# Four small loads moved from ScalarE's queue to SyncE's, the sink loads moved behind a weight slab, and one projection tile computed in another order

## The reference

```python
for i in range(DEPTH):                      # 2 layers
    h = rmsnorm(x, norm_w[i])
    if i % 2 == 0:                          # attention, 4 key/value groups of 4 heads
        q, k, v, g = split(h @ w_attn_in)   # q, k are normalised per head
        p = softmax_with_sink(q @ k.T, attn_sinks)
        out = (p @ v * silu(g)) @ w_attn_out
    else:                                   # SSM: uses a_log, dt_bias, d_skip
        out = mamba2(h, ..., dt_bias, a_log, d_skip, ...) @ w_ssm_out
    x = x + out
```

## Time and profile before

| | before |
|---|---|
| median of 3 runs (range) | 1024.51 us (1024.32 to 1026.81) |
| profiled execution | 1027.62 us |
| span, first to last instruction | 1024.7 us |
| PE matmul busy | 980.9 us (96%) |
| DVE, ACT, POOL busy | 581.2, 466.9, 365.8 us |
| mean granted TensorE clock | 0.988 of full speed |

### The profile page before, as it was taken

One profiled execution on the slowest core, in us unless ns is written; L12 is line 12 of the kernel. 1 busy time (PEld: TensorE's weight loads), 2 busy tenths in 40 slices (PEclk: granted clock), 3 DMA queues, 4 the chain that ended last, 5 costly groups with the idle time before them and its releaser, 6 DMA issues.

```text
span 1024.7 us, 18539 instructions
## 1 busy us (share of the span) xinstructions
PE 980.9 (96%) x7372; PEld 902.1 (88%) x7372; DVE 581.2 (57%) x1433; ACT 466.9 (46%) x819; POOL 365.8 (36%) x275
## 2 busy tenths in 40 slices
PE   8999999999999999999997999999999999999988
PEld 7988899989998899978986889998799978997867
DVE  5114431354224431356685787966889577986772
ACT  5324623365134623366444364343552445526453
POOL 4240233113330233115533335534354244443610
PEclk9999999999999999999998999999999999999999
DMA  6351221242233222101423715247242563416303
GB/s 198 101 155 62 83 83 53 85 157 65 66 103 141 84 83 59 73 21 42 148 86 87 226 44 157 83 111 205 62 136 84 148 186 82 137 47 207 92 11 98
DMA packets 144117, 106.35 MB, mean 104 GB/s; under 512 B 10258, under 2 KB 135364, under 8 KB 143840
## 3 DMA queue, kind: packets, MB, share of 16 engines
q1 hardware_dynamic: 115032, 92.24, 29.0%
q10 hardware_dynamic: 29000, 12.94, 4.8%
HBM read 92.44 MB, written 16.79 MB: 107 GB/s over the span
## 4 chain that ended last, share of the span: by engine, by line
PE 79%; DVE 10%; issue 4%; DMA 3%; ACT 2%; POOL 2%; ACTq 0%; SPq 0%; DVEq 0%; POOLq 0%
PE pp L1202 19%; PE pp L1204 19%; PE pp L1203 18%; PE pS L1318 3%; DMA w_raw_buf<-in_w_attn_in 2%; PE pS L1542 2%; DVE cv L1914 2%; PE pO L1364 1%; PE pO L1363 1%; PE pO L1535 1%; PE pO L1531 1%; PE pT_ L1521 1%; PE pO L1482 1%; POOL w_lo_raw L608 1%; DVE z L2056 1%
## 5 line engine op out<-in xcount | busy, mean ns | idle before, releaser
L608 POOL TENSOR_TENSOR w_lo_buf<-w_raw_buf,w_hi_buf 128x512 fp32r<-128x512 f32 x214 | 288.0, 1377 | 503.0 <-ACT w_hi_buf L689 272.0
L1202 PE MATMUL pp<-h_hi,w_hi_buf 128*128 128x280 f32 (+1 forms) x1248 | 379.6, 304 | 7.8 <-POOL w_lo_buf L608 2.9
L1204 PE MATMUL pp<-h_hi,w_lo_buf 128*128 128x280 f32 (+1 forms) x1248 | 364.1, 292 | 0.0
L1203 PE MATMUL pp<-h_lo,w_hi_buf 128*128 128x280 f32 (+1 forms) x1248 | 363.5, 291 | 0.0
L1202 PEld LDWEIGHTS pp<-h_hi,w_hi_buf 128*128 128x128 f32 x1248 | 236.7, 190 | 19.0 <-issue 11.7
L1203 PEld LDWEIGHTS pp<-h_lo,w_hi_buf 128*128 128x128 f32 x1248 | 236.4, 189 | 4.6 <-issue 4.1
L1204 PEld LDWEIGHTS pp<-h_hi,w_lo_buf 128*128 128x128 f32 x1248 | 236.4, 189 | 0.0
L689 ACT ACTIVATE w_hi_buf<-w_raw_buf 128x2048 fp32r<-128x2048 f32 (+1 forms) x55 | 104.1, 1892 | 38.7 <-DMA w_raw_buf<-in_w_ssm_in 16.9
L1700 DVE TENSOR_TENSOR x<-x,pp 128x272 f32<-128x272 f32 (+3 forms) x128 | 56.4, 440 | 80.3 <-PE pp L1204 79.4
L1202 PE MATMUL pp<-og_hi,w_hi_buf 128*128 128x280 f32 (+2 forms) x256 | 76.2, 298 | 1.8 <-DVE og_lo L1821 1.1
L1204 PE MATMUL pp<-og_hi,w_lo_buf 128*128 128x280 f32 (+2 forms) x256 | 75.2, 294 | 0.0
(11 more groups left out here) (334 smaller groups left out, 1730.0 us busy)
## 6 DMA issues: line engine op xcount, KB each, us to landing
w_raw_buf<-in_w_attn_in SPq DMA_DIRECT2D x16, 1024.0 KB, 5.2
w_raw_buf<-in_w_ssm_in SPq DMA_DIRECT2D x16, 1024.0 KB, 5.4
w_raw_buf<-in_w_attn_out SPq DMA_DIRECT2D x8, 1024.0 KB, 5.1
s_in<-in_state_ssm SPq DMA_DIRECT2D x32, 256.0 KB, 4.2
out<-s_in SPq DMA_DIRECT2D x32, 256.0 KB, 3.0
seg<-a_scratch ACTq DMA_DIRECT2D x16, 512.0 KB, 4.1
w_raw_buf<-in_w_ssm_out SPq DMA_DIRECT2D x8, 1024.0 KB, 5.6
w_raw_buf<-in_w_attn_in SPq DMA_DIRECT2D x8, 512.0 KB, 5.9
```

Source lines behind the costliest of these rows:

```text
L608: ins = pool.tensor_tensor(low_buf(n)[:, piece], raw[n % RAW_SLOTS][:, piece], high_buf(n)[:, piece].bitcast(F32), ALU.subtract)
L1202: pe.matmul(dst, hi[:, k, cols], a_hi[:, k, tk], start=(k == 0), stop=False)
L1203: pe.matmul(dst, hi[:, k, cols], a_lo[:, k, tk], start=False, stop=False)
L1204: mm = pe.matmul(dst, lo[:, k, cols], a_hi[:, k, tk], start=False, stop=(k == depth - 1))
```

## The change

The two loads of `d_skip` and those of `dt_bias` and `a_log` leave ACT's program and stand in SP's, in the loop over the groups at group 1, behind the load of slab 7. On SP, the cached values of group 0 and slab 3 are now ahead of the sinks and sink rows. On POOL, the subtraction of the value columns of slab 0 waits for all eight blocks of activations. On PE, the first half of the value tile runs its 16 matmuls with the high weight first, then waits for the low part, then runs the 8 matmuls with the low weight.

```diff
+            def load_ssm_scalars():
+                for half in range(2):
+                    src = d_skip[0, :].rearrange("(t e) -> e t", e=2)[half]
+                    sp.dma_start(dskip[64 * half:64 * half + 64, :], src.partition_broadcast(64),
+                                 allow_slow_non_contiguous=True).then_inc(s_late, 16)
+                sp.dma_start(dtb[:, :], dt_bias.rearrange("a h -> h a"),
+                             allow_slow_non_contiguous=True).then_inc(s_late, 16)
+                sp.dma_start(alog[:, :], a_log.rearrange("a h -> h a"),
+                             allow_slow_non_contiguous=True).then_inc(s_late, 16)
...
+            load_cache(0, 1)
+            load_slabs(4)
             sp.dma_start(sinks[:, :], attn_sinks[0, :].partition_broadcast(P)).then_inc(s_small, 16)
...
-            load_cache(0, 1)
 
             for s in range(GROUPS):
+                if s == 1:
+                    load_slabs(slab_no[("out", 0, 1)] + 1)
+                    load_ssm_scalars()
                 load_slabs(slab_no[("gate", s, 1)] + 1)
...
                 if i:
-                    pool.wait_ge(h_ready, KM - 2)
+                    pool.wait_ge(h_ready, KM)
...
-            for half in range(2):
-                src = d_skip[0, :].rearrange("(t e) -> e t", e=2)[half]
-                act.dma_start(dskip[64 * half:64 * half + 64, :], src.partition_broadcast(64),
-                              allow_slow_non_contiguous=True).then_inc(s_late, 16)
-            act.dma_start(dtb[:, :], dt_bias.rearrange("a h -> h a"),
-                          allow_slow_non_contiguous=True).then_inc(s_late, 16)
-            act.dma_start(alog[:, :], a_log.rearrange("a h -> h a"),
-                          allow_slow_non_contiguous=True).then_inc(s_late, 16)
             norm_scale(0)
...
                 if (kind, s, tile) == ("kv", 0, 1):
                     pe.wait_ge(w_hi, 1)
-                    pe.wait_ge(w_lo, 1)
                     pe.wait_ge(x_ready, KM)
...
-                for k in range(depth):
+                high_first = (kind, s, tile, half) == ("kv", 0, 1, 0)
+                if high_first:
+                    for k in range(depth):
+                        pe.matmul(dst, hi[:, k, cols], a_hi[:, k, tk], start=(k == 0), stop=False)
+                        pe.matmul(dst, hi[:, k, cols], a_lo[:, k, tk], start=False, stop=False)
+                    pe.wait_ge(w_lo, 1)
+                    for k in range(depth):
+                        mm = pe.matmul(dst, lo[:, k, cols], a_hi[:, k, tk], start=False, stop=(k == depth - 1))
+                for k in range(0 if high_first else depth):
```

## The result

| | before | after |
|---|---|---|
| median (range): 4 runs before, 3 after | 1024.84 us (1024.32 to 1026.81) | 1013.84 us (1013.11 to 1014.47) |
| ratio (95% interval) | 1 | 0.9893 (0.9877 to 0.9908) |
| profiled execution, its span | 1027.62, 1024.7 us | 1013.84, 1011.5 us |
| mean granted TensorE clock | 0.988 | 0.993 |

A further run of the changed kernel took 2417.61 us, more than twice the others for a reason that the record does not show, and is left out of the table (with it the median is 1014.15). The forecast was 1015.5 us, with a spread of 1013.5 to 1018 and a range that goes to 1020.

A forecast was written before the change was run, and what follows sets the result against it. PE was taken as the bound from 72 us on, with gains only before 68 us: 2.28 + 1.49 + 3.08 + 1.33 + 0.86 = 9.04 us off the 1024.5 median gives 1015.5, spread 1013.5 to 1018, range to 1020.

The forecast's parts named there:

- Gap 1: PE's 2.16 us idle before the last activation block at 24.27; POOL waiting for eight blocks was to gain 2.28 us.
- High-first: Value tile's high-weight matmuls first: costs nothing and hides POOL's later low part, for which PE would otherwise wait 1.7 us.
- The slow half tile: Half tile from 25.18 to 29.86, behind the first gap, at the lower clock: 4.68 us would become 3.19, gain 1.49.
- Gap 2: PE's 2.92 us wait at 52.90 for slab 2's low part; moving the small loads off ACT was to gain 3.08.
- the slow stretch: Twelve matmuls from 52.90 to 55.83, behind the wait for slab 2: 2.93 us would become 1.60, gain 1.33.
- gap 3: PE's 0.70 us wait at 67.51 for slab 3's low part; slab 3 ahead of the sinks was to gain 0.86.
- The rival that queues take turns: Slab 2's late landing is not d_skip's doing, so only 0.86 us is won: 1025.6 us; chance 0.06.
- The rival that the small loads block slab 8: On SP the small loads land one after another, making slab 8 43.4 us late: 1058.9 us, slower; chance 0.05.
- the cover of 37.0: SP's queue may be held from 107.5 to 144.5 us before PE needs slab 8; each microsecond beyond costs one.
- The clock falling anyway: Rival: the start still has gaps and slow matmuls cost 1.49 or also 1.33: 1017.0 or 1018.3 us; chance 0.11.

The follow-up runs named there:

- run seven: Changed kernel, but POOL starts the value columns' low part after six blocks, as before: 1018.38 us, ratio 0.9933.
- Run six: Changed kernel, but PE waits for the low part before the value tile's first matmul, products in the old order: 1017.31 us, ratio 0.9926.
- run three: Kernel before with only SP's order changed, cached values and slab 3 ahead of the sinks: 1023.95 us, ratio 0.9989.
- run one: Kernel before with only the four small loads moved from ACT to SP behind slab 7: 1018.45 us, ratio 0.9932.
- nine: Changed kernel with only dt_bias and a_log (64 elements) back on ACT's queue: 1013.55 us, one run.
- twelve: Changed kernel once more, unchanged, against the kernel before: 1014.97 us, 5 runs, ratio 0.9909.
- run four: Kernel before once more, unchanged, for a second profile: 1023.96 us, 10 runs, ratio 0.9995.
- two: Kernel before with only the POOL wait and the PE product order changed, loads as before: 1025.77 us, ratio 1.0008.
- five: Changed kernel with both d_skip loads back on ACT's queue at their old place: 1023.38 us, ratio 0.9995 to the kernel before.
- ten: Changed kernel with the first d_skip load (1024 elements) back on ACT's queue, the second on SP: 1015.96 us, one run.
- run eight: Changed kernel with the two d_skip loads issued three times in a row behind slab 7: 1042.9 us, ratio 1.0179.

## Why the prediction was right

**Gap 1 (2.28 us): right.** PE enters the value tile at 22.56 instead of 25.18, 2.62 earlier; run seven puts the cause on POOL beside DVE. The 0.34 more is in the block itself: without waiting for DVE it takes PE 0.78 us, where I took the 0.91 of a block behind a gap, and the one before it went the same way.

**High-first (no cost, against 1.7): right.** POOL has the low part at 21.45 + 2.54 = 23.99, sooner than my 24.6 because POOL too is faster alone; PE asks for it at 24.60. Run six shows the 1.6 us that the wait would have cost.

**The slow half tile (1.49): the size was right, the cause is open.** The half tile takes 25.73 - 22.56 = 3.17 us after, 4.68 before. I put the slow clock down to gap 1. But the same gap is followed by the lower level in the kernel before, in its repeat and in run three, and by 1.00 in runs one and seven. Run three has a gap 2 of 3.18 us without it, too. A gap of over 2 us can have it behind it and need not. In the three with it `d_skip` was under way on ACT's queue, in the two without it was not; whether that is more than chance in five profiles was not tried. So 1.49 was won against the trace that I had, and is not a fixed price of a gap; nor is the 1.33 behind gap 2. In the kernel as changed there is no such gap left, and no profile of it (runs nine to twelve among them) shows a lower clock before 60 us.

**Gap 2, the slow stretch and gap 3 (3.08, 1.33, 0.86): right in size, gap 3 in part by luck and for another cause.** The third query tile begins at 45.58, 7.32 earlier than before; 4.13 of it had been won by the sums of squares (29.86 to 25.73), so gap 2 gave 3.19. From there to the marker another 9.60 - 7.32 = 2.28 is won, against 1.33 + 0.86 = 2.19. Together the five terms are 9.04 by the forecast and 9.60 measured; the gain in the medians, 11.0, is 2.0 above the forecast, and 1.4 of that lie behind the marker, where I had forecast nothing.

The 0.86 of gap 3 was there to win in the first profile of the kernel before and not in its second (run four). And I put it down to the sinks ahead of slab 3. What delayed slab 3 were the elements of `d_skip` again, by way of the issues that stand ahead of it in SP's program: with the loads alone moved (run one), the sinks stay where they were, their issue falls from 7.64 to 0.43 us, and ACT rounds slab 3 at 50.52 without a wait, instead of at 60.39 after 8.99 us of it. Beside the moved loads, no run shows that the new place of the sinks wins anything.

**The edits are not a sum of separate ones.** Alone they gave 6.4 (one), nothing (two) and 0.9 or nothing (three); together 8.7 to 11.0 by the medians. What the POOL and PE edits win reaches the end only when slab 2 is there in time; the prediction's order of steps (slab 2 at 41.5, asked for at 46.05) had this in it, and runs two and five are its test.

**The rival that queues take turns** fell. Runs five, ten and nine set the hold by the count of elements on ACT's queue: 20.0 us, 10.2 us, none. It came from the Trainium skill ("DMA: Bandwidth & Descriptors", section "Queues, rings and completion order"), by which a DMA engine drains a packet from one queue and then turns to the next. No trace here contradicts that for the engines, which were 95% idle, and where both queues have packets they do move side by side (39.5 to 41 us before); but until then SP's loads did not reach them, and the rule as a forecast of the time, 1025.6, would have been wrong by 11.8 us. I gave it 0.06; the table by queue, above, would have let me give it less.

**The rival that the small loads block slab 8** names a true mechanism with too high a price: the loads do stand ahead of a slab, at about 10 ns an element (22.8 us from the first issue to slab 8's first bytes, while slab 7 still moved for the first four) and not the 22 from which it decides. At three times the elements it decides: by the 61.3 us hold less the cover of 37.0, PE should lose 24.3, and by slab 8's first tile it had lost 25.2. The cover of 37.0 us was a good reading of the earlier trace rows.

**The clock falling anyway** did not happen in a profile of the changed kernel ahead of the marker. That kernel has no gap over 0.5 us there, so it gives this rival no test; in runs six and seven, which put a gap of 1.34 and of 2.15 us back into the start, the clock behind it is 1.00.

## What to carry to other kernels

Count the pieces of a load, not its bytes: 2048 pieces of 4 bytes hold the loads issued behind them for some 20 us, where 16 KB in 128 pieces take 2.8. On ACT's queue they held SP's loads too; on SP's queue they held SP's own, and no run has a load on ACT's queue meanwhile. In the trace it shows as empty GB/s with one queue's small packets and no row for the other, and as issues of 7 us and more on the other engine; look there when a large load lands late, and move such a load to a place where the next large one is not asked for in that time. Before adding up edits ahead of a common wait, work out which of them the wait lets through.

## What the runs showed of the hardware that was not expected

- The hold goes by the element and is much the same from either queue: 10.2 us for 1024, 19.7 and 20.0 for 2048 on ACT's queue, 22.8 for 2112 and 61.3 for 6208 on SP's (there with some four us of slab 7 in it); 9.6 to 10.8 ns each, at 4 to 5% of the engines' time. In the midst of it the packets come at 9.4 ns on ACT's queue (1494 in 14 us, run five) and 9.2 on SP's (1083 in 10 us, run eight, 120 to 130 us).
- Behind the elements it is the next issues that get long, on the other engine too: SP's took 7.45 and 8.41 us in run five instead of 0.43 and 0.37, while the two issues of `d_skip` took ACT 1.41 together.
- In run eight PE stops for 5.66 us inside a tile. Just behind 139 us the instruction queue has its only packet between 120 and 145, and PE goes on at 141.39. That its next instructions were late because their load stood behind the elements too would fit; it is argued, not shown, and other instruction packets came through the hold without a stop.
- POOL and DVE slow each other: DVE's 0.50 and 0.80 us become 1.54 and 1.72 beside POOL, POOL's 2.54 becomes 3.18.
- The lower clock level is not bound to a gap of a given length: 2.13 (run one) and 2.15 us (seven) without it, 2.13 (run four) and 2.16 (before, run three) with it.
